# Earlier signal and moved copies in the recurrent pairs, one negation per unit, gates behind transposes

## Time and profile before

| | |
|---|---|
| time, median of 3 | 3466.57 us |
| time of the profiled execution | 3465.34 us |
| its span | 3463.4 us |
| busy PE, DVE, ACT, POOL | 3247.9, 2009.3, 1055.9, 1674.6 us |
| mean granted clock of TensorE | 0.978 |

### The profile page before, as it was taken

The page is one execution under the profiler, slowest core; times in us unless marked ns, Lnnn a source line. Parts: engine busy times, 40 slices in busy tenths (PEclk is TensorE's granted clock), DMA queues, the critical chain, the costliest instruction groups (busy, mean ns, idle before and its releaser), DMA issues.

```text
span 3463.4 us, 52617 instructions
## 1 busy us (share of the span) xinstructions
PE 3247.9 (94%) x19342; PEld 2566.8 (74%) x19342; DVE 2009.3 (58%) x2727; ACT 1055.9 (30%) x1970; POOL 1674.6 (48%) x1323
## 2 busy tenths in 40 slices
PE   7988999899999999899999999999989899999999
PEld 4756777777888887576777788877657677788887
DVE  5647677765566545624645666656552635586556
ACT  2142333322121113543534321112551535231112
POOL 3423322225476664244344666655226263576665
PEclk9998999999999999999999999999999999999999
DMA  5431111112232221012121232222112121222222
GB/s 206 165 121 44 44 38 38 38 38 67 91 100 96 95 95 61 31 55 67 54 69 62 85 98 92 97 86 80 36 37 92 37 86 44 85 90 93 97 96 92
DMA packets 71657, 268.36 MB, mean 77 GB/s; under 512 B 7840, under 2 KB 7968, under 8 KB 68384
## 3 DMA queue, kind: packets, MB, share of 16 engines
q1 hardware_dynamic: 69152, 260.73, 22.6%
q10 hardware_dynamic: 2304, 4.83, 0.4%
HBM read 263.44 MB, written 2.10 MB: 77 GB/s over the span
## 4 chain that ended last, share of the span: by engine, by line
PE 75%; DVE 16%; ACT 5%; issue 2%; DMA 1%; POOL 0%; DVEq 0%; SPq 0%; ACTq 0%; POOLq 0%
PE psum_a L574 10%; PE psum_a L578 10%; PE psum_a L577 10%; PE psum_d L637 5%; PE psum_d L574 5%; PE psum_d L577 5%; PE psum_d L578 5%; PE psum_a L729 3%; PE psum_d L832 2%; PE psum_a L600 2%; PE psum_a L603 2%; PE psum_a L604 2%; PE psum_a L759 1%; PE psum_a L763 1%; PE psum_a L762 1%
## 5 line engine op out<-in xcount | busy, mean ns | idle before, releaser
L3297 POOL TENSOR_TENSOR w_lo<-raw,w_hi 128x1024 fp32r<-128x1024 f32 x440 | 1114.3, 2532 | 36.7
L3293 POOL TENSOR_TENSOR mark<-mark 128x1 f32<-128x1 f32 x438 | 105.5, 241 | 1712.7 <-PE psum_a L574 866.7
L574 PE MATMUL psum_a<-h_hi,w_hi 128*128 128x512 f32 x1712 | 676.7, 395 | 0.0
L578 PE MATMUL psum_a<-h_hi,w_lo 128*128 128x512 f32 x1712 | 669.1, 391 | 0.0
L577 PE MATMUL psum_a<-h_lo,w_hi 128*128 128x512 f32 x1712 | 668.9, 391 | 0.0
L3294 POOL TENSOR_SCALAR w_hi<-raw 128x1024 fp32r<-128x1024 f32 x440 | 471.2, 1071 | 33.8 <-DMA raw<-in_weights 33.8
L574 PEld LDWEIGHTS psum_a<-h_hi,w_hi 128*128 128x128 f32 x1712 | 323.1, 189 | 78.1 <-issue 11.2
L577 PEld LDWEIGHTS psum_a<-h_lo,w_hi 128*128 128x128 f32 x1712 | 323.1, 189 | 68.0 <-issue 1.9
L578 PEld LDWEIGHTS psum_a<-h_hi,w_lo 128*128 128x128 f32 x1712 | 322.7, 189 | 68.0
L574 PE MATMUL psum_d<-split,w_hi 128*128 128x512 f32 x848 | 331.1, 390 | 9.5 <-DVE x L3044 6.7
L577 PE MATMUL psum_d<-split,w_hi 128*128 128x512 f32 x848 | 330.0, 389 | 0.0
(11 more groups left out here) (394 smaller groups left out, 5713.9 us busy)
## 6 DMA issues: line engine op xcount, KB each, us to landing
raw<-in_weights SPq DMA_DIRECT2D x440, 512.0 KB, 3.4
plain<-in_ada SPq DMA_DIRECT2D x20, 1024.0 KB, 7.2
arena<-in_ada SPq DMA_DIRECT2D x4, 1024.0 KB, 17.5
x<-in_x SPq DMA_DIRECT2D x1, 2048.0 KB, 12.8
x<-in_x ACTq DMA_DIRECT2D x1, 2048.0 KB, 10.7
out<-x SPq DMA_DIRECT2D x8, 256.0 KB, 3.7
arena<-in_pe ACTq DMA_DIRECT2D x2, 512.0 KB, 3.6
const<-in_const ACTq DMA_DIRECT2D x1, 906.0 KB, 9.4
```

What stands on the lines that cost most here:

```text
L574: m = pe.eng.matmul(dst, wh, hi(t), start=t == 0, stop=False)
L578: m = pe.eng.matmul(dst, wl, hi(t), start=False, stop=t == k - 1)
L3293: eng.tensor_tensor(b.mark[:, 1:2], b.mark[:, 0:1], b.mark[:, 0:1], ALU.add)
L3297: eng.tensor_tensor(lo, b.raw[:, s], hi.bitcast(F32), ALU.subtract).then_inc(sig["w_ready"], 1)
```

## The change

1. `dve_rwkv_prepare` raises `rk_ready` behind `R_BH`; `AR[...,1]`, `R_KH` and `E` move to a new function called in level k = 1, behind the two mask multiplications and ahead of the addition of `normal`.
2. The diagonal becomes a tile of ring a, and ACT copies its two halves between the two corners.
3. In the differential attention each unit has its own negation and its own `s_ready`; the squares come two units later.
4. In the rows, PE makes the transposes ahead of `extra`, and ACT copies them ahead of the gate.

```diff
@@ pe_rows
-        if extra:
-            extra(p)
         if 0 <= p - 2 < len(pairs):
             ... transposes of pair p - 2
+        if extra:
+            extra(p)
@@ pe_rwkv, diagonal
-        tl = pe.tile("d")
+        tl = pe.tile("a")
...
-        m.then_inc(tl.full, pe.up("full_d"))
+        m.then_inc(tl.full, pe.up("full_a"))
@@ act_rwkv
-    for part, dst in ((slice(HD, P), b.R_Z[HD:P]), (slice(0, HD), b.R_TF[j % 2][0:HD, :, HD:])):
-        a.eng.wait_ge(a.sem["full_a"], a.due("full_a"))
-        a.eng.wait_ge(a.sem[a.last], a.own())
-        a.eng.activation(dst, a.bank()[part].rearrange("p (u t) -> p u t", u=8), ACT.Copy)\
...
+    a.eng.activation(b.R_Z[lower], eight(a.bank()[lower]), ACT.Copy).then_inc(a.sem["free_a"], a.up("free_a"))
+    a.eng.wait_ge(a.sem["full_a"], a.due("full_a"))
+    ps = eight(a.bank())
...
+    a.eng.activation(TF[lower, :, lower], ps[lower], ACT.Copy).then_inc(a.sem["act_step"], a.up("act_step"))
...
+    a.eng.activation(TF[upper, :, upper], ps[upper], ACT.Copy).then_inc(a.sem["free_a"], a.up("free_a"))
+    a.eng.wait_ge(a.sem["full_a"], a.due("full_a"))
...
+    a.eng.activation(TF[upper, :, lower], eight(a.bank()[upper]), ACT.Copy).then_inc(a.sem["free_a"], a.up("free_a"))
@@ act_rows: "if gates: gates(p)" moves behind the copies of pair p - 2
@@ act_attention
-            if s % 2:
-                a.eng.wait_ge(a.sem["s_ready"], a.due("s_ready"))
+            a.eng.wait_ge(a.sem["s_ready"], a.due("s_ready"))
...
-        if 0 <= s - lag - 3 and units[s - lag - 3].v:
-            act_output_square(a, units[s - lag - 3])
-    for u in units[-2:]:
+        if 0 <= s - lag - 5 and units[s - lag - 5].v:
+            act_output_square(a, units[s - lag - 5])
+    for u in units[-4:]:
@@ dve_rwkv_prepare
-    v.eng.tensor_tensor(b.R_BH, b.R_AA, b.R_CUM, ALU.mult).then_inc(v.sem["dve_step"], v.up("dve_step"))
+    v.eng.tensor_tensor(b.R_BH, b.R_AA, b.R_CUM, ALU.mult).then_inc(v.sem["rk_ready"], v.up("rk_ready"))
+def dve_rwkv_receptance(v, j):
...
     v.eng.tensor_tensor(AR[:, :, 1], chunks(b.R_R), b.R_PB[:, :, 1:], ALU.mult)\
...
     v.eng.tensor_tensor(b.R_KH, b.R_KP, b.R_CUM, ALU.mult).then_inc(v.sem["dve_step"], v.up("dve_step"))
...
     v.eng.tensor_tensor(E, b.R_PB[:, 0:3, P], b.col[:, 169:172], ALU.mult)\
-        .then_inc(v.sem["rk_ready"], v.up("rk_ready"))
+        .then_inc(v.sem["dve_step"], v.up("dve_step"))
@@ dve_rwkv
+        if k == 1:
+            dve_rwkv_receptance(v, j)
...
-    v.eng.wait_ge(v.sem["full_d"], v.due("full_d"))
-    ps, step = eight(v.bank()), "dve_step"
-    for r, cols in zip(ROWS, ROWS):
-        v.eng.wait_ge(v.sem[v.last], v.own())
-        v.eng.tensor_copy(TF[r, :, cols], ps[r]).then_inc(v.sem[step], v.up(step))
-        step = "free_d"
@@ dve_attention
-            if s % 2:
-                v.eng.wait_ge(v.sem[v.last], v.own())
-                v.eng.tensor_scalar(u.two_neg, u.two_top, -u.scale, None, ALU.mult).then_inc(v.sem["s_ready"], v.up("s_ready"))
+            v.eng.wait_ge(v.sem[v.last], v.own())
+            v.eng.tensor_scalar(u.neg, u.top, -u.scale, None, ALU.mult).then_inc(v.sem["s_ready"], v.up("s_ready"))
```

More of the change, by code:

```diff
@@ L1751, in act_rwkv @@
         act_rwkv_centered(a)
-    for part, dst in ((slice(HD, P), b.R_Z[HD:P]), (slice(0, HD), b.R_TF[j % 2][0:HD, :, HD:])):
-        a.eng.wait_ge(a.sem["full_a"], a.due("full_a"))
-        a.eng.wait_ge(a.sem[a.last], a.own())
-        a.eng.activation(dst, a.bank()[part].rearrange("p (u t) -> p u t", u=8), ACT.Copy)\
-            .then_inc(a.sem["free_a"], a.up("free_a"))
+    eight = lambda ps: ps.rearrange("p (u t) -> p u t", u=8)
+    upper, lower = ROWS
+    TF = b.R_TF[j % 2]
+    a.eng.wait_ge(a.sem["full_a"], a.due("full_a"))
+    a.eng.wait_ge(a.sem[a.last], a.own())
+    a.eng.activation(b.R_Z[lower], eight(a.bank()[lower]), ACT.Copy).then_inc(a.sem["free_a"], a.up("free_a"))
+    a.eng.wait_ge(a.sem["full_a"], a.due("full_a"))
+    ps = eight(a.bank())
+    a.eng.wait_ge(a.sem[a.last], a.own())
+    a.eng.activation(TF[lower, :, lower], ps[lower], ACT.Copy).then_inc(a.sem["act_step"], a.up("act_step"))
+    a.eng.wait_ge(a.sem[a.last], a.own())
+    a.eng.activation(TF[upper, :, upper], ps[upper], ACT.Copy).then_inc(a.sem["free_a"], a.up("free_a"))
+    a.eng.wait_ge(a.sem["full_a"], a.due("full_a"))
+    a.eng.wait_ge(a.sem[a.last], a.own())
+    a.eng.activation(TF[upper, :, lower], eight(a.bank()[upper]), ACT.Copy).then_inc(a.sem["free_a"], a.up("free_a"))
     if j:
@@ L1864, in act_rows @@
                 a.eng.activation(st.sunk, st.sunk, ACT.Exp).then_inc(a.sem["sunk"], a.up("sunk"))
-        if gates:
-            gates(p)
         if 0 <= p - 2 < len(pairs):
@@ L1873, in act_rows @@
                         .then_inc(a.sem["free_a"], a.up("free_a"))
+        if gates:
+            gates(p)
         for f in range(len(steps) // 2):
@@ L2257, in columns @@
         if n % 2:
-            u.two_top, u.two_inv = b.col[:, 119 + n % 4:121 + n % 4], b.col[:, n % 32 - 1:n % 32 + 1]
-            u.two_neg, u.two_sum = b.col[:, c - 2:c + 2:2], b.col[:, c - 1:c + 3:2]
+            u.two_inv, u.two_sum = b.col[:, n % 32 - 1:n % 32 + 1], b.col[:, c - 1:c + 3:2]
     return units
@@ L2457, in dve_rwkv_prepare @@
 def dve_rwkv_prepare(v, j):
-    b, AR, E = v.b, v.b.R_AR[j % 2], v.b.R_E[j % 2]
+    b, AR = v.b, v.b.R_AR[j % 2]
     v.eng.wait_ge(v.sem["decays"], v.due("decays"))
@@ L2468, in dve_rwkv_prepare @@
     v.eng.wait_ge(v.sem[v.last], v.own())
-    v.eng.tensor_tensor(b.R_BH, b.R_AA, b.R_CUM, ALU.mult).then_inc(v.sem["dve_step"], v.up("dve_step"))
+    v.eng.tensor_tensor(b.R_BH, b.R_AA, b.R_CUM, ALU.mult).then_inc(v.sem["rk_ready"], v.up("rk_ready"))
+def dve_rwkv_receptance(v, j):
+    b, AR, E = v.b, v.b.R_AR[j % 2], v.b.R_E[j % 2]
+    chunks = lambda t: t.rearrange("p (c n) -> p c n", c=NQ)
     v.eng.wait_ge(v.sem[v.last], v.own())
```

## The result

The kernel after takes 3420.01 us, the median of four runs (3419.04 to 3424.06); the kernel before took 3465.84 us in the same comparison (3461.83 to 3469.8). The ratio is 0.987, with a 95% interval of 0.9853 to 0.9887: 39 to 51 us faster. The profiled execution fell from 3465.34 to 3424.06 us, its span from 3463.4 to 3422.1, so 41.3 us are in the two traces. I had forecast 3435 us and no less than 3424. The direction was right; the gain was larger than the sum of 31.5 said. The profiled execution is the slowest of the four, 4 us over their median, and what the other three gained beyond it is in no trace.

A forecast was written before the change was run, and what follows sets the result against it. TensorE, busy 94% of the span, was taken as the bound, so only its waits counted. Terms -7.0 - 8.1 - 8.4 - 8.0 = -31.5 us gave a forecast of 3435 us; 8 in 10 range 3424 to 3454.

The forecast's parts named there:

- Held by the splits: Recurrent pairs, level 1: the three moved operations meet a POOL split in each pair; total -16.9 us, 3450 us; chance 0.13.
- DVE bounds the differential attention: Differential attention: DVE bounds the loop, so the negation per unit ends at +6.4 us; total -16.7, 3450 us; chance 0.12.
- The waits do not go: Recurrent pairs: PE waits there for something else, level 1 still costs 3.0 us; total -13.4, 3453 us; chance 0.08.
- The exponentials lose their cover: Attention rows: transposes ahead of gates wait for exponentials, 1.45 us per stage; total +25.8 us, 3492 us; chance 0.05.

The follow-up runs named there:

- the repetition: The kernel before, unchanged, run once more for one profiled execution: 3463.24 us.
- parts 1 and 2 alone: Kernel before with only the earlier signal, three operations moved to level 1, and the diagonal on ACT in ring a: 3446.71 against 3466.39 us.
- the experiment on the place: Kernel after with the three moved operations left right behind the signal instead of in level 1: 3435.17 us, ratio to the kernel before 0.991.
- part 2 alone: Kernel before with only the diagonal's two copies on ACT and its bank in ring a: 3465.18 against 3466.56 us.

## Why the forecast was too small

Stage by stage, the terms of the sum against the two traces (us, rounded):

| stage | sum | traces |
|---|---|---|
| up to pair 0's first products | -3.2 | -5.7 |
| the eight pairs | -13.4 | -14.4 |
| latent attention, both layers | -3.9 | -2.7 |
| differential attention | -8.4 | -12.4 |
| window attention | -2.6 | -6.3 |
| all | -31.5 | -41.3 |

The mechanisms came as told; sizes failed: that of part 3, that of part 4 in the windows, and the clock, which was left out everywhere but in pair 6. The prediction had named a total under -40 as the sign of a step mis-sized by half. By medians the miss is 14.3 us; the 4 us beyond these traces stay open.

**The largest step that failed is the size of part 3.** "Some waits are shorter than 0.8 and DVE has one more small operation per two units, about 0.2 us; I take 0.6 for each place" gave -8.4; it measured -12.1 to -12.4. The 0.86 us that I had worked out from the earlier trace rows was the right number. In layer 1 the seven steps by which value products came earlier were 0.88, 0.36, 0.82, 0.82, 0.87, 1.13 and 0.81 us, 5.7 of the stage's 6.2; the rest came ahead of the first. The extra negation (0.15 us) costs nothing: the second maximum and its negation are done at 1637.99, while ACT has its first exponential and then the copy, until 1638.48. The discount had no row behind it. This is 4.0 of the 9.8 us that the sum missed.

**The clock was counted in one place.** I took 2.7 us in pair 6, where I had seen the stop. The trace has 8.6 us less loss: 4.3 up to pair 0, 2.5 in the pairs and 1.7 in each window, less 1.7 lost anew before the second latent stage of layer 1. The part up to pair 0, 2.5 us of time, may be chance, as the repetition shows (there 5.0 us more of loss in an unchanged program). The windows' part is not: they gave 6.3 us instead of 2.6. Of the 3.1 in each, 0.9 is the fall, if it is worth what it was in the repetition; 1.7 are the two waits of the earlier trace rows, which I had discounted to 1.3; and some 0.5 is under no wait that the profile names.

**Part 1** went step by step: pair 0 from 4.76 to 3.13 (1.63, forecast 1.67), pairs 4 to 7 without a wait, pair 6 at clock 1, level 1 with +2.5 us (forecast 3.0) and pair 2's operation held until 0.55 us behind the split (forecast 0.6). Pair 1's wait of 0.75 was not foreseen; with parts 1 and 2 alone it was not there. The unchanged kernel has one of 0.65 in one execution and none in the other, so a wait of this size there can come and go by itself. The Trainium skill, "SBUF — State Buffer", section "Who interferes with whom", says that a DVE instruction with two SBUF inputs contends with a GpSimd instruction that reads SBUF. The rows of pair 2, and of pair 4 in the experiment on the place, agree: both operations lasted until the split's end or just behind it. The rival made of it, a split in every pair, did not come: one pair in eight met one in full, one in part. It held for the old place instead, ahead of the pair, where L1178 then waited in seven of eight pairs (12.2 us).

**Part 2** gave its -8.1 in the sum and -1.4 by itself. The prediction priced it as if it stood alone and said only that the next signal comes forward; it did not say that without part 1 the signal would be late by as much, nor that an earlier PE brings the splits forward onto the preparation. The total of the two parts, -15.1, was near the -14.4 of the pairs and 1.6 of pair 0, because the two were made together. ACT's copies take 0.59 us each, as the rows had it:

```profile
453.85 0.59 ACT L1761 ACTIVATE arena<-psum_a 64x512 f32<-64x512 f32 x1 [0.18 <-PE psum_a L1206]
454.47 0.59 ACT L1763 ACTIVATE arena<-psum_a 64x512 f32<-64x512 f32 x1
```

The Trainium skill, "ScalarE: Activation LUTs", section "Rules for kernel authors", sends `relu`, `max`, `min`, `add` and `mul` to VectorE, with a reason given for bf16; float32 copies from PSUM are not in its list. Here they take 0.59 us on ACT and took 0.70 on DVE, where they also stood in the queue that PE needs.

**Part 4** in the latent attention: the four waits of 0.98 went, and each value product came 0.8 to 0.9 us earlier (3.4 us), but the stages that hold them gained only 2.7 in both layers. Most of the difference is 0.9 us lost again before the second latent stage of layer 1, where the clock lost 1.7 more. In the first block 1.15 of the forecast 1.5 came.

**Rivals.** Held by the splits: refuted for level 1, which lost 2.5 us, though splits made the waits of part 2 alone. DVE bounds the differential attention: refuted by the 12.4. The waits do not go: refuted for both parts together, true of part 2 alone. The exponentials lose their cover: refuted, the window stages became shorter in every kernel with part 4.

The parts measured singly add to 33.0 us, with 1 and 2 as one to 44.2, against 45.8 for the whole. The intervals are several us wide, so that the last two agree is in part luck.

## What to carry to other kernels

Two waits in one loop can cover each other: before a part is priced alone, ask what PE would meet next if it came earlier by that wait, and what follows PE (here POOL's splits) and would come earlier with it. An operation ahead of what PE waits for should be there only if it is needed there; here two such operations cost some 10 us. Where a row gives a delay and its chain is fixed, take the whole of it, and keep the doubt for the range.

## What the runs showed of the chip

The granted clock is not fixed by the program alone: the kernel before, run twice, lost 11.4 and 15.9 us to it in the first 280 us, and one window stage had a fall in one execution and none in the other. It makes single profiles differ by 2 us in a stage whose instructions are the same. And a 128x3 operation of DVE, 0.16 us when alone, took 2.18 us behind a running split of POOL: its size says nothing about its cost there.
